# Residual rows kept in DRAM during the experts, and a sixth expert buffer, in a hybrid decoder step

## The reference

```
proj   = rms_norm(x) @ w_in                  # 1024 x 3072: q, k, v, h, B, C
att    = dilated attention(q, k, v)          # 8 heads of 64, prompt and cache
conv   = B * conv3(C * h)                    # 512 channels
h      = x + [norm(att) | norm(conv)] @ w_out
m      = rms_norm(h, g_ffn)
group  = top1(m @ w_router_group)            # 4 groups of 8 experts
e1, e2 = top2 inside the group               # so 2 x 1056 = 2112 rows in all
h     += sum_k w_k * (silu(m @ w_gate[e]) * (m @ w_up[e])) @ w_down[e]
h     += (p @ w_ple_proj) * sigmoid(rms_norm(h, g_ple) @ w_ple_gate)
```

## Time and profile before

| | us |
|---|---|
| median of the runs | 1253.34 |
| the profiled execution | 1244.78 |
| its span, first to last instruction | 1243.1 |
| projection | 0 to 205 |
| prompt attention | 205 to 330 |
| convolution and sample attention | 330 to 608 |
| output projection and router | 608 to 765 |
| lists and first rows | 765 to 780 |
| experts, 23 blocks | 780 to 1080 |
| final stage | 1080 to 1243 |

### The profile page before, as it was taken

The page is one execution under the profiler, slowest core; times in us unless marked ns, Lnnn a source line. Parts: engine busy times, 40 slices in busy tenths (PEclk is TensorE's granted clock), DMA queues, the critical chain, the costliest instruction groups (busy, mean ns, idle before and its releaser), DMA issues.

```text
span 1243.1 us, 14883 instructions
## 1 busy us (share of the span) xinstructions
PE 1163.9 (94%) x5726; PEld 606.6 (49%) x5726; DVE 411.5 (33%) x972; ACT 326.9 (26%) x643; POOL 151.5 (12%) x147
## 2 busy tenths in 40 slices
PE   6999997999999999999999993989999899899997
PEld 3444443666666665555555552434333334344443
DVE  1222223566642232231365566331111111023443
ACT  2232312777721121110011111011111111244443
POOL 1011100012220000000111112621111110000000
PEclk9999998899999999999999996889999899899999
DMA  8211013001083526335471113789999999732321
GB/s 307 56 51 51 24 61 108 11 30 34 2 256 99 149 81 169 119 119 185 129 275 53 66 51 130 296 306 359 418 392 422 406 390 382 304 120 69 122 88 39
DMA packets 66420, 209.24 MB, mean 168 GB/s; under 512 B 17950, under 2 KB 31678, under 8 KB 50480
## 3 DMA queue, kind: packets, MB, share of 16 engines
q1 hardware_dynamic: 55296, 181.93, 41.0%
q0 software_dynamic: 10528, 26.37, 5.7%
q10 hardware_dynamic: 528, 0.00, 0.0%
HBM read 189.68 MB, written 25.42 MB: 173 GB/s over the span
## 4 chain that ended last, share of the span: by engine, by line
PE 85%; DMA 7%; DVE 3%; ACT 2%; issue 1%; SPq 0%; POOL 0%; ACTq 0%; POOLq 0%; DVEq 0%
PE pair L2031 14%; PE pair L1819 13%; PE pair L2195 10%; PE pair L2094 9%; PE pair L2302 9%; DMA R<-in_w_up 5%; PE pair L2217 5%; PE pair L1875 3%; PE pair L1888 3%; PE pair L1901 3%; PE pair L2283 2%; PE pair L2182 1%; PE pair L2123 1%; PE pair L1950 1%; PE pair L1967 1%
## 5 line engine op out<-in xcount | busy, mean ns | idle before, releaser
L2195 PE MATMUL pair<-R 128*32 128x512 f32 (+2 forms) x896 | 172.5, 618 | 13.2 <-DMA R<-in_w_up 11.1
L2031 PE MATMUL pair<-R 128*128 128x352 f32 x576 | 181.9, 470 | 0.0
L1819 PE MATMUL pair<-R 128*128 128x512 f32 x384 | 169.2, 597 | 3.2 <-DMA R<-in_w_in 3.2
L2031 PEld LDWEIGHTS pair<-R 128*128 128x128 f32 x576 | 108.3, 193 | 59.6 <-issue 7.3
L1819 PEld LDWEIGHTS pair<-R 128*128 128x128 f32 x384 | 72.3, 192 | 89.2 <-issue 89.2
L2094 PE MATMUL pair<-R 128*128 128x512 f32 x256 | 113.8, 597 | 0.0
L2302 PE MATMUL pair<-R 128*128 128x512 f32 x256 | 111.5, 593 | 1.7 <-ACT R L1142 1.7
L2195 PEld LDWEIGHTS pair<-R 128*32 128x32 f32 (+2 forms) x896 | 58.8, 132 | 110.3 <-issue 106.0
L1647 DVE TENSOR_TENSOR R<-pair,R 128x256 f32<-128x256 f32 x23 | 9.8, 425 | 238.4 <-ACT R L1090 238.4
L2217 PE MATMUL pair<-R,bias_s 128*32 128x512 f32 (+2 forms) x448 | 83.4, 595 | 0.5 <-ACT bias_s L1094 0.5
L2302 PEld LDWEIGHTS pair<-R 128*128 128x128 f32 x256 | 47.9, 190 | 59.2 <-issue 59.1
(11 more groups left out here) (285 smaller groups left out, 1272.6 us busy)
## 6 DMA issues: line engine op xcount, KB each, us to landing
R<-in_w_gate SPq DMA_DIRECT2D x32, 1024.0 KB, 12.2
R<-in_w_up SPq DMA_DIRECT2D x32, 1024.0 KB, 15.3
R<-in_w_down SPq DMA_DIRECT2D x32, 1024.0 KB, 11.6
R<-in_x_prompt SPq DMA_DIRECT2D x16, 512.0 KB, 3.5
R<-in_cache_k SPq DMA_DIRECT2D x8, 1024.0 KB, 5.6
R<-in_cache_v SPq DMA_DIRECT2D x8, 1024.0 KB, 5.3
R<-y_dram SPq DMA_DIRECT2D x16, 512.0 KB, 4.5
R<-in_w_in SPq DMA_DIRECT2D x3, 2048.0 KB, 16.6
```

The source lines that it names most:

```text
L1819: last = mm(bk[4 + part][0:n, :], xTs[a.u][:, c, 0:n], wA[:, c, AD * part:AD * part + AD], start=(c == 0), stop=(c == DC - 1))
L2031: last = mm(bk[b][:, 0:n], wB[q % 2][:, c, which, :], xT[:, c, lo:lo + n], start=(c == 0), stop=(c == DC - 1))
L2195: last = mm(bk[2 + u][r, :].rearrange("p (w f) -> p w f", w=2), xgT[u][:, c, r], wgu[s][:, :, c, :], start=(c == 0), stop=(c == DC - 1))
```

## The change

`residual_conv` writes its sum back into `x_re`. SP stores it to a new DRAM tensor `h_dram` and loads it in the final stage into three buffers. The freed SBUF holds a sixth expert buffer. Four experts are loaded in the output projection. The static experts are six: 0 to 3 as one T, 4 and 5 as a P, so that four blocks are static; the plan of the others changes, and there are 21 blocks. Lists are fetched four at a time. `g_ple` is loaded during the experts into the place of `g_ffn`. Other places in SBUF move, and some semaphores are shared.

```diff
-NSTAT = 4
-PLAN = "PFTPFTPFTPFPP"
+NSTAT = 6
+NSTATB = 4
+NSLOT = 6
+PLAN = "FFPFFTPPPPPTP"
-    blocks = [Blk((e,), FULL, e) for e in range(NSTAT)]
+    blocks = [Blk((1 + j, 0), TRI, None) for j in range(3)] + [Blk((4, 5), PAIR, None)]
-    slot, before, count = [0, 3, 1, 2, 4], [None] * (NSTAT + 1), [1] * (NSTAT + 1)
+    slot, before, count = [0, 3, 2, 5, 1, 4], [None] * NSTAT, [1] * NSTAT
-        s = min((s for s in holder if s < 4 or l < NE - 4), key=lambda s: (last[holder[s]], holder[s]))
+        s = min((s for s in holder if s not in (1, 4) or l < NE - 5), key=lambda s: (last[holder[s]], holder[s]))
...
         def load_x2(i):
             if i >= 2:
-                sp.wait_ge(S("h_done"), pieces(i - 1))
+                sp.wait_ge(S(f"h_out{a.u}"), 16 * (i // 2))
+                sp.wait_ge(S("hg_done"), i - 1)
+                sp.wait_ge(S("ssh"), i - 1)
+        def store_h(i):
+            a = turned(i)
+            sp.wait_ge(S("h_done"), pieces(i + 1))
+            sp.dma_start(h_dram[P * a.t:P * a.t + a.rows, :], x_re[a.u][0:a.rows, :]).then_inc(S(f"h_out{a.u}"), 16)
         for l in range(2):
             load_wide(l, LSLOT[l])
             load_down(l, LSLOT[l])
-        for i in range(2, TILES):
-            load_x2(i)
+        for i in range(TILES):
+            store_h(i)
+            if i + 2 < TILES:
+                load_x2(i + 2)
+            if i < 2:
+                load_wide(2 + i, LSLOT[2 + i])
+                load_down(2 + i, LSLOT[2 + i])
         sp.wait_ge(S("oC_full"), halves(TILES))
-        load_wide(2, LSLOT[2])
-        load_down(2, LSLOT[2])
-        sp.wait_ge(S("lg_full"), TILES)
         for u in range(2):
             sp.wait_ge(S(f"rows_in{u}"), 16)
-        load_wide(3, LSLOT[3])
-        load_down(3, LSLOT[3])
+        load_wide(4, LSLOT[4])
+        load_down(4, LSLOT[4])
+        sp.wait_ge(S("idx_done"), 2)
+        load_wide(5, LSLOT[5])
...
-        for l in range(NSTAT + 1, NE):
+        for l in range(NSTAT, NE):
             e = expert(l)
             sp.wait_ge(S("gu_full"), LBEFORE[l] + 1)
             load_wide(e, LSLOT[l])
             sp.wait_ge(S("y_full"), 2 * LBEFORE[l] + 2)
             load_down(e, LSLOT[l])
-            if l == NSTAT + 1:
+            if l == NSTAT:
                 sp.wait_ge(S("routed"), 1)
-                load_down(fifth, 4)
+                load_down(5, LSLOT[5])
+                sp.dma_start(gple, I["g_ple"][0:1, :].broadcast_to([P, D])).then_inc(S("wrt_in"), 16)
...
+        def load_h(t):
+            if t >= 3:
+                sp.wait_ge(S("out_done"), t - 2)
+            sp.dma_start(h[t % 3][0:a.rows, :], h_dram[P * t:P * t + a.rows, :]).then_inc(S(f"ring_in{t % 3}"), 16)
...
-            if n < 2:
-                for k in range(NSTAT + n, NBM, 2):
+            if n == 0:
+                for k in range(NSTATB, NSTATB + 4):
                     fetch(k)
-            else:
+            if n >= 2:
                 scatter(n - 2, n % 2, lists[0:CAP, 2 * n - 3:2 * n - 2])
+            if first:
+                for k in range(n + 6, min(n + 10, NBM)):
+                    fetch(k)
...
-        act.dma_start(lists[:, 0:2 * NSTAT].rearrange("p (e c) -> p e c", c=2),
-                      list_dram.rearrange("(e r) c -> r e c", r=LROWS)[0:CAP, 0:NSTAT, :]).then_inc(S("static_in"), 16)
+        act.dma_start(lists[0:96, 0:6].rearrange("p (e c) -> p e c", c=2),
+                      list_dram.rearrange("(e r) c -> r e c", r=LROWS)[0:96, 1:4, :]).then_inc(S("small_in"), 16)
+        act.dma_start(lists[96:128, 0:6].rearrange("p (j c) -> p j c", c=2),
+                      list_dram[0:96, :].rearrange("(j r) c -> r j c", j=3)).then_inc(S("small_in"), 16)
+        for k in range(2):
+            act.dma_start(lists[64 * k:64 * k + 64, 6:8], list_dram[LROWS * (4 + k):LROWS * (4 + k) + 64, :]).then_inc(S("small_in"), 16)
```

More of the change, by code:

```diff
@@ L162, in item @@
     return i % 3, 32 * (i // 3 + 1)
+RING_USED = tuple(32 * len(ITEMS[k::3]) for k in range(3))
 SAMPLE_PARTS = (("squares",), ("keys", 0, 0), ("keys", 0, 1), ("score", 0), ("keys", 1, 0), ("keys", 1, 1), ("score", 1),
@@ L387, in _build @@
     gffn = view(R2, 8192, D)
-    gple = view(R2, 9216, D)
-    w_rt = view(R1, 9216, DC, RG)
+    gple = view(R2, 8192, D)
+    w_rt = view(R1, 8448, DC, RG)
     x_re = [view(R2, 10240 + 1024 * s, D) for s in range(2)]
[L391 to L394, removed]
+    m_st = [view(R2, 9216, D), view(bias, 0, D)]
+    mT = [view(R1, 6144 + 1024 * s, DC, P) for s in range(2)]
+    junkE = R2[:, 12288:12288 + 512].bitcast(BF16)
     def scratch(at, end, region=R1):
@@ L451, in _build @@
     xgT = [view(R3, 2048 + DC * CAP * s, DC, CAP) for s in range(2)]
-    hT = [view(bias_s, 2 * CAP * s, 2, CAP) for s in range(2)]
+    hT = [view(bias, 2 * CAP * s, 2, CAP) for s in range(2)]
     yo = [R2[0:CAP, 10240 + 1024 * s:10240 + 1024 * (s + 1)] for s in range(2)]
@@ L456, in _build @@
     w_pg = [view(R2, 1024 * c, D) for c in range(DC)]
+    h = [view(R1, 6144 + 1024 * s, D) for s in range(3)]
     y0, y1, hn = ([view(R1, at + 1024 * s, D) for s in range(2)] for at in (9216, 11264, 15360))
@@ L698, in _, with load_y, store @@
             sp.dma_start(w_pg[c], I["w_ple_gate"][0].rearrange("(p c) n -> p c n", c=DC)[:, c, :]).then_inc(S("wpg_in"), 16)
+        def load_h(t):
+            a = fixed(t)
+            if t >= 3:
+                sp.wait_ge(S("out_done"), t - 2)
+            sp.dma_start(h[t % 3][0:a.rows, :], h_dram[P * t:P * t + a.rows, :]).then_inc(S(f"ring_in{t % 3}"), 16)
+        def load_y(t):
+            a = fixed(t)
+            if t >= 2:
+                sp.wait_ge(S("h2_done"), t - 1)
+            for k, y in ((0, y0), (1, y1)):
+                sp.dma_start(y[a.u][0:a.rows, :], y_dram[TOK * k + P * t:TOK * k + P * t + a.rows, :]).then_inc(S(f"in{a.u}"), 16)
+        def store(t):
+            a = fixed(t)
+            sp.wait_ge(S("out_done"), t + 1)
+            sp.dma_start(rows_of(O[0], O[1], a), ot[a.u][0:a.rows, :]).then_inc(S(f"fin_out{a.u}"), 16)
+        for u in range(2):
+            sp.wait_ge(S(f"h_out{u}"), 16 * USES[u])
+        load_h(0)
+        load_h(1)
         for u in range(2):
             sp.wait_ge(S(f"rows_out{u}"), 16 * ((NBM + 1 - u) // 2))
[L702 to L723, removed]
+        load_y(0)
+        for t in range(TILES):
+            if t + 1 < TILES:
+                load_y(t + 1)
+            if t + 2 < TILES:
+                load_h(t + 2)
+            if t >= 1:
+                store(t - 1)
+        store(PT)
         sp.wait_ge(S("fin_out0"), 16 * USES[0])
@@ L1081, in _ @@
         act.wait_ge(S("list_out"), 16 * 2 * TILES)
-        act.dma_start(lists[:, 0:2 * NSTAT].rearrange("p (e c) -> p e c", c=2),
-                      list_dram.rearrange("(e r) c -> r e c", r=LROWS)[0:CAP, 0:NSTAT, :]).then_inc(S("static_in"), 16)
+        act.dma_start(lists[0:96, 0:6].rearrange("p (e c) -> p e c", c=2),
[4 more added lines that the diff above has]
+            act.dma_start(lists[64 * k:64 * k + 64, 6:8], list_dram[LROWS * (4 + k):LROWS * (4 + k) + 64, :]).then_inc(S("small_in"), 16)
+        for u in range(2):
+            act.wait_ge(S(f"h_out{u}"), 16 * USES[u])
         def gate_rows(n, u):
```

77 lines of the change are left out of this document (41 added, 36 removed).

## The result

The changed kernel took 1240.6 us (median of 4 runs, 1236.45 to 1242.2), the kernel before 1254.11 in the same comparison (1252.66 to 1256.44): ratio 0.9881, interval 0.9852 to 0.9911. Two later comparisons, on different chips, gave 0.9978 (0.9961 to 0.9996) and 0.9895 (0.9876 to 0.9914). The changed kernel is steady over the three (1240.6, 1241.89, 1243.34 us); the kernel before is not (1254.11, 1244.66, 1254.67, and 1245.92 in a fourth comparison). The profiled execution took 1239.8 us (span 1238.1) against 1244.78 (1243.1), so the two profiles show 5.0 us of difference, not 13.

What follows compares the result with a forecast made beforehand. Transfers were taken to set the experts' stage's end, by little, and TensorE the rest. Terms 0.5 + 1.3 + 0.4 - 6.4 - 3 + 3.8 = -3.4 us, from 1253.34 to 1249.9 us; 8-in-10 range 1239 to 1257.

Steps and rivals of the forecast that it cites:

- Output projection (+0.5): Prologue: x loaded after the sum's store, behind experts 2 and 3, just fits; +0.5 us, bounds 0 and +10.
- Lists (+1.3): Prologue: four list DMAs issued in series on ScalarE's queue delay the first gather; +1.3 us, bounds -0.5 and +6.0.
- `spill_blocks` (+0.4): Prologue: two more small subtractions in spill_blocks, which holds the fourth block; +0.4 us.
- Bytes: Experts' stage: one load ahead, with g_ple added, leaves 2.6 MB less to bring at 412 GB/s; -6.4 us.
- full queue: Experts' stage, 835 to 870 us: one buffer more queues an additional load; -3 us, range 0 to -4.3.
- dry end: Experts' late blocks: SP's in-order issue leaves the queue dry after a run of pairs; +3.8 us, from -3.7 to +8.
- Two blocks fewer (0, since they save no bytes): Experts' stage: the two blocks that are gone save no bytes, since padded rows are not moved.
- Lists by fours (0): Fetching lists four at a time has a block's time to run beside TensorE; 0 us.
- The queue stays full: Rival for the experts' stage: six buffers keep loads ahead of TensorE to the end; -12.2 us, 1241.1 us, chance 0.22.
- Nothing gained: Rival: pairs starve TensorE; slow products and dry end eat the load ahead; +1 to -2, 1253 us, chance 0.13.
- Stores before loads: Rival in the output projection: late x delays TensorE; +9.5 for +0.5, 1259 us; chance 0.13 together with late lists.
- no spill ran: Rival: data overflow experts 4 and 5's 64 rows, running 32 spill blocks, some 390 us; chance 0.02.

Runs made afterwards that it cites:

- the kernel with both mends: The changed kernel with SP issuing weights as buffers come free and plan PFTPFFTFPPPPP, all pairs at the end: 1230.27 us, ratio 0.9881 to the kernel before.

## Why the prediction was right or wrong

**Sign and size.** Faster, as forecast. The sum said -3.4 us on the profiled execution; it measured -5.0, and -2.8 in the timed comparison with the least difference. Against the runs shown before, the forecast of 1249.9 lies 9.3 us above the measured 1240.6, though inside the range. The step that failed there is the transfer of -3.4 us from the profiled execution (1244.78) to a median 8.6 us higher. The kernel before has something in some comparisons that its profile doesn't show and that the changed kernel lacks; what it is stays open.

**Output projection (+0.5).** 607.62 to 752.13 in the chain against 608.89 to 751.72: +1.7, and none of it comes from the change. It lies in one product of 16 matmuls that starts at 617.21, before the first store, and takes 8.58 us where the kernel before took 6.88: the granted clock was 0.51 from 619 to 621, its lower level, against 1.00. In its second execution the unchanged kernel took 8.58 us there too. TensorE had been busy throughout; what lowers the clock stays open. From 627.97 (before: 627.55) to 752.13 (751.72) the two kernels keep the same distance, 0.4 us, and TensorE waits 0.3 us for VectorE there in both. x came at 646.54 and 659.59 (said: 647.5 and 661). So the stores and the loads cost 0, where the sum had 0.5, and the run with the loads moved away agrees.

**Lists (+1.3).** From the first of these DMAs to the gather it took 4.47 us against 2.99: +1.5. The four overlap, as the row of one issue led to expect; the upper bound of a full landing each is out. The Trainium skill's rule to coalesce small transfers (DMA: Bandwidth & Descriptors, "Rules for kernel authors") holds here in direction alone, with 0.5 us for each one more.

**`spill_blocks` (+0.4).** Its own part came as said: from the second block's start to the fourth's it is 27.7 us against 27.4. But the way from the first block to the fourth grew by 1.5 us, and the sum lacked a term. ScalarE's table load, before and after:

```profile
770.72 1.28 ACT L1090 ACT_TABLE_LOAD   x1 [5.20 <-DMA list_dram<-code,pos_i]
```

```profile
790.38 1.28 ACT L1124 ACT_TABLE_LOAD   x1 [24.77 <-PE pair L2232]
```

In the kernel before it came right behind the DMA issue; now it stands behind the wait for the first products, and TensorE waits for it: from the end of those products to the second block's start it takes 2.1 us in both executions of the kernel before and 3.5 in all three of the changed one. Two waits (`h_out`) now stand between that DMA and the activation, and I take them for what moved it. I counted the DMAs added to ScalarE's queue and not its waits. Whether a table load ahead of them gets the 1.28 us back wasn't tried.

**Bytes, full queue, dry end (-6.4, -3, +3.8).** Together -5.6; measured -6.9 from the fourth block to the last. The single signs came as said: 416 and 418 GB/s from 835 to 870, no up matrix in the chain before block 13, the hollow of 282 GB/s, load 28's down matrix 13.7 us after block 17 began (said: about 12), the last block at 1057.93 (said: 1059). The sizes did not, and that the sum is near is in part luck:

- Bytes: from 819 us to the last block's start the kernel before moved 396 GB/s for 243.1 us, the changed one 391 for 238.9. That is 2.9 MB less, 7.0 us at 412 GB/s, where the sum had 2.6 MB and 6.4.
- Full queue: (416 - 353) x 15 + (418 - 368) x 20 = 1.9 MB, 4.7 us, where I took 3 (3.8 us against the second execution of the kernel before).
- Dry end: (382 - 282) x 30 = 3.0 MB, 7.3 us, where I took 3.8. That SP's order makes it is confirmed by its removal (5.4 us of stage).

No run takes the byte term away: the kernel with one load fewer in the output projection and the one with five buffers in turn both ask for six experts before `routed`, and the latter moves 371 GB/s for 251.9 us from 819 on, the same 93.4 MB as the changed kernel. What was wrong is the worth of the buffer. I had priced it as one load ahead plus a little in 35 us, 9.4 us together. Refusing it its later loads cost 20.8 us, a part of it through the three buffers that were left to the last five loads, and all of the change but these later loads was 18.0 us slower than the kernel before. The gain is the small difference of the two, and my sum held neither.

**Two blocks fewer (0, since they save no bytes).** The bytes are the same (26.37 MB), as said, but the price is not shown to be nothing: the plan with 23 blocks took 10.3 us more, a part of it through a hollow of its own. TensorE's side of the stage adds up as well: two blocks of 12.1 us less, 12.9 us more of waits for up matrices (24.0 for 11.1) and about 4.7 us more of slow products behind them (9.96, 9.39 and 9.01 us for blocks 13, 15 and 17, in place of 7.1; before one of 9.47) make -6.6, an estimate from these rows. So most of the two blocks' time went into waits, not all of it.

**Lists by fours (0).** In the changed kernel they cost nothing that the trace shows. That their absence costs 16 us was in no case of mine.

**Rivals.** "The queue stays full" was right up to 1000 us and wrong after. It needed SP's order mended, and with the pairs last as well the stage fell to 265.4, below what that rival had priced (281.7 less about 14). "Nothing gained" is not far from what the second chip shows, 2.8 us faster with an interval that ends at 0.9996; its own sum, 2.2 - 6.4 + 0 + 6, is +1.8 and not "+1 to -2". Stores before loads did not make it slower, and no spill ran.

## What to carry to other kernels

Where one queue issues all loads in program order, each of its waits is a wait of all that stand behind it: list them, sort them by when they are met, and move the latest (here a wait for a flag, 9 us of stage, and the pairing of up and down matrix, 5 us) before buying another buffer. A buffer is worth what it keeps queued over the whole stage, which a count of loads ahead at its start does not give. When a matrix comes late, count the slow products behind a long wait with the wait itself. And when waits are put into an engine's program, look at what stood next in it, table loads included.

## What the runs showed of the hardware that was not expected

Transfers held 417 to 422 GB/s on one core for 150 us (850 to 1000, in the kernel with both mends). TensorE's granted clock was 0.50 behind a wait of 4.60 us and 1.00 behind one of 1.28, and the same products took 9.96 and 7.09 us; it also fell without a wait, to 0.51 from 619 to 621 in the changed kernel and to 0.54 from 623 to 625 in one of two executions of the kernel before. Seventeen indirect DMAs issued by POOL in a row, 1.3 us apart, went with a 15.6 us hole on TensorE and SP whose releaser the trace does not name, where runs of 4 and of 10 had none. The same kernel before took 1244.7 to 1245.9 us in two comparisons and 1254.1 to 1254.7 in two others, while the changed one stayed within 1240.6 and 1243.3. The mean granted clock does not tell the two levels of time apart: executions with 0.972 took 1247.5 us on one chip and 1254.4 on another.
